# One decoder kernel: memory rows first in the DMA queues, the first projection's features turned between weight splits, and four stages without unused products

## The chip, the core and the metric

The kernel runs on one core of a Trainium2 chip. The metric is the device time of one execution, in microseconds (us). The engines are TensorE (PE in the profile; PEld is its weight load), VectorE (DVE), ScalarE (ACT), GpSimd (POOL) and SyncE (SP). SP does nothing here but issue the large transfers; ACT and POOL issue a few at the start. The kernel before takes 1924.37 us, the median of three runs (1923.10 to 1926.65).

## The reference

One sequence of 256 tokens of 1024 features, in float32, goes through four layers. What the change touches is the first of them, and the memory keys and values that two later layers read:

```
mod = silu(c) @ ada_w[layer] + ada_b[layer]          # (1024) x (1024 x 6144), two layers
sh1, sc1, g1, sh2, sc2, g2 = split(mod, 6)
h = rms_norm(x, norm1_g) * (1 + sc1) + sh1
proj = h @ even_w_in                                 # (256 x 1024) x (1024 x 3584)
rq, rk, rv, rg, aq, ak, av = split(proj)             # retention and attention inputs
rq, rk = rotary(rq), rotary(rk)
x = x + g1 * (concat(retention, attention) @ even_w_out)
...
mem_n = rms_norm(mem, mem_norm_g[l])                 # 256 memory rows, two later layers
k, v = mem_n @ ca_wk[l], mem_n @ ca_wv[l]            # (256 x 1024) x (1024 x 256) each
```

After it come a mixture of 16 experts in 4 groups, a stick-breaking attention layer with its experts, a layer with forget-gated and compressed sparse attention ("b0" in the code), a differential attention layer ("b1"), and in the last two a memory cross attention and a SwiGLU feed-forward.

## The kernel before

**Split products.** The large products are done in three passes. Each weight tile of 128 x 2048 is copied by ACT to a rounded high part (`weights_high`, line 1520), DVE subtracts that from the tile to give the low part (`weights_low`, line 2071), both in two halves of 1024 columns, and TensorE multiplies high by high, high by low and low by high (lines 722 to 724). The features are split the same way. A group of 512 output columns takes two weight tiles and 48 products of 512 columns: 24 for the features 0 to 511 (first tile, both token blocks), then 24 for the rest (second tile).

**The ring.** Weight tiles come through a ring of three slots, in two halves of 512 KB. SP asks for a half once the tile three places earlier in the plan has been split by DVE (or summed, see below), half by half; its instructions run in order, so a half that has to wait holds all later ones. The high and low parts have three slots of their own, freed when TensorE has used them.

**The modulation.** Twenty-four blocks of 512 columns of `ada_w` pass through the same ring, two tiles each. DVE sums them over the features with eight instructions per block (`ada_steps`, lines 2335 and 2342) and TensorE finishes the sum over partitions with products against ones (lines 855 and 858). Three blocks are done on TensorE (line 875). In `project`, DVE's code for the first projection puts the eight steps of a block ahead of the splits of groups 0, 1, 4, 5 and twice 6 (`ADA_EVEN`).

**The start.** ACT asks for c, the memory rows, three small constant tensors and x; POOL asks for eight small tensors, the first two gate bias rows (128 x 2048) among them. SP alternates one block of `ada_w` with one of the four memory weights. DVE sums block 0 (eight steps), then scales the memory rows by their root; TensorE transposes them for layer 0, computes its keys, transposes them for layer 1, and computes the other three products, each with one block's modulation behind it. Then ACT and DVE split both tiles of the first group, and x is transposed, scaled and shifted into features (`take_turned("a0h1", ...)`), two feature blocks at a time in turns between PE, ACT and DVE. POOL asks for the attention bias (128 x 3072), the rotary table (128 x 256) and the retention decay (128 x 1536) when the last memory values have been copied. DVE needs the rotary table at line 2231, after group 2 of the projection and the modulation behind it.

**Unused products.** `stay_busy` (line 739) multiplies a constant tile by itself into a bank that nobody reads, where TensorE would wait. It is called in many stages; each product is 128 x 512.

Of the kernel before, what the change touches and what calls it, by code (L numbers as in the profile page):

```python
# [15 lines left out]
KD = D // 128  # L16
# [164 lines left out]
def build(nc, a, out):  # L181
# [3 lines left out]
    with ctx:  # L185
# [247 lines left out]
        class Pairs:  # L433


            def __init__(self, name, P=None):

                self.name, self.wide = name, name[:2] == "ca"
                self.keys = [256, 256] if self.wide else [128, 256]
                self.width = sum(self.keys)  # L440
                self.first, self.first_out, count, self.out_banks = {
                    "a0": (0, 0, 4, [2, 3]), "b0": (4, 4, 12, [6, 7]), "ca0": (16, 12, 2, [6, 7]),
                    "ca1": (18, 14, 2, [6, 7])}[name]
                self.score_sets = 1 if name == "a0" else 2
                self.scale = 1.0 if name == "a0" else HD ** -0.5
                self.idle = {"a0": (8, 0, 0, 0), "b0": (5, 0, 0, 0)}.get(name, (4, 11, 0, 0))
                self.items = [self.item(i, P) for i in range(count)]
# [92 lines left out]
        CONSTS, MORE, LATE = 16 * 3, 16 * 8, 16 * 3  # L540
# [5 lines left out]
        def _(eng):  # L546
# [104 lines left out]
            for l in range(2):  # L651
                for i, w in enumerate(("ca_wk_2", "ca_wv_2")):
                    ada()
                    eng.dma_start(MEM_WEIGHTS[2 * l + i], cols(a[w][l], 0, 256)).then_inc(kv_loaded[2 * l + i], 16)
# [45 lines left out]
        def _(eng):  # L700
# [444 lines left out]
            turns_taken("mem0")  # L1145
            mem_keys(0)
            turn("mem1", lambda i, tb: NB[:, tb, i * 128:(i + 1) * 128])
            turns_taken("mem1")
            modulation((2, 3))
            mem_values(0)  # L1150
            modulation((2, 3))
            mem_keys(1)
            modulation((2, 3))
            mem_values(1)
            modulation((2, 3))
# [3 lines left out]
            turn_normed("a0h1", busy=(9, 3, 3, 3))  # L1159
# [30 lines left out]
            def in_even(j):  # L1190

                if j in (1, 2, 5):
                    modulation((2, 3))
                if j == 3:
                    eng.wait_ge(mod_taken, 6)
                    stay_busy(2, 4)
                    eng.wait_ge(a0_rotated, 1)
                    for x in range(4):
                        turn_a0(x, 256 * x)
                if j == 5:  # L1200
                    eng.wait_ge(a0_normed, 1)
# [120 lines left out]
            def in_ev(j):  # L1322
# [4 lines left out]
                if j == 4:  # L1327
                    eng.wait_ge(gates_copied, 1)
                    eng.wait_ge(cmp_dve, 1)
                    for i, t in enumerate(st["cmp"]):  # L1330
                        stay_busy(0, 4)
                        loaded(t)
                        w1 = slot(t).rearrange("p (k n) -> p k n", k=16)
                        for k in range(16):
                            mm = eng.matmul(B[2 + i][:, 0:31], w1[:, k, :], XS[i][:, k, :], start=(k == 0), stop=(k == 15))
                        mm.then_inc(*used.up())
# [160 lines left out]
        def _(eng):  # L1497
# [9 lines left out]
            eng.dma_start(X[:, :, :], a["x"].rearrange("b (t p) d -> p (b t) d", p=128)).then_inc(x_loaded, 16)  # L1507
# [22 lines left out]
            def take_turned(name, dst, affine=None, split=False):  # L1530

                first, items = turns[name]
                for i in range(items):
# [12 lines left out]
                    if split and i % 2 == 1:  # L1546
                        high_features(i - 1, 2, (x + 1) // 2)

# [275 lines left out]
            take_chunks(st["kv0"][0], lambda c: MK[:, 0, c, :])  # L1824
# [6 lines left out]
            take_chunks(st["kv0"][1], lambda c: MV[:, 0, c, :])  # L1831
            take_chunks(st["kv1"][0], lambda c: MK[:, 1, c, :])
            take_chunks(st["kv1"][1], lambda c: MV[:, 1, c, :])
            splits(tiles[st["even_in"][0][0][0]]["split"] + 2)
            eng.wait_ge(scales_ready, 1)
            take_turned("a0h1", feature, lambda i: (SCL[:, 0, i:i + 1], MOD[:, 0, i:i + 1]), True)
# [215 lines left out]
        def _(eng):  # L2052
# [36 lines left out]
            def take_turned(name, dst, affine=None, split=False):  # L2089
# [258 lines left out]
            def ada_take(j, banks, room=None):  # L2348

                l, i = j // 12, j % 12  # L2350
                if j == 16:
                    eng.wait_ge(gates_loaded, 16)
# [230 lines left out]
            ada_steps(KD)  # L2583
# [4 lines left out]
            ada_steps(KD)  # L2588
            take_turned("mem1", lambda i: MEM_HT[1][:, i, :], lambda i: (GM[:, 11, i:i + 1], None))
            ada_steps(KD)  # L2590
            ada_take(0, (2, 3))
# [8 lines left out]
            take_turned("a0h1", feature, lambda i: (SCL[:, 0, i:i + 1], MOD[:, 0, i:i + 1]), True)  # L2600
# [379 lines left out]
        def _(eng):  # L2980

            for dst, src in ((AG[:, :], a["qk_gains"]), (GB[:, 0:2, :], a["gate_bias"][0:2].partition_broadcast(128)),
                             (RW[:, :, :], cols(a["router_w"], 0, 16)), (RB[:, :], a["router_b"].partition_broadcast(128)),
# [3 lines left out]
            eng.wait_ge(copied["act"], chunks[st["kv1"][1][-1]]["done"])  # L2987
# [116 lines left out]
```

## Times and profile before

| what | us |
|---|---|
| median of three runs | 1924.37 |
| profiled execution, own time | 1924.36 |
| its span | 1922.6 |
| TensorE busy | 1788.5 (93%) |
| VectorE busy | 1264.9 (66%) |
| ScalarE busy | 1073.1 (56%) |
| unused products (line 739), 350 of them | 97.9 |

The profiled execution's own time is the median's. An instruction's start is counted from the start of the span. A busy TensorE is not one at its peak: matmuls overlap, so a product's cost in a row of products is the distance of two starts. TensorE's granted clock has two levels, 1.00 (2.4 GHz) and 0.50 (1.2 GHz).

### The profile page before, as it was taken

What the parts mean: (1) busy time and instruction counts of PE and PEld (TensorE: products, weight loads), DVE (VectorE), ACT (ScalarE), POOL (GpSimd) and SP (SyncE); (2) the same over time, 40 slices, a digit from 0 to 9 for tenths busy, and PEclk for the clock granted to TensorE, in tenths of its full rate; (3) what the DMA queues carried; (4) which work ended last, traced back from release to release, by engine and by line L of the source; (5) the groups of instructions that cost most, each with busy time, mean ns of one, the idle gap of its engine ahead of it and who ended that gap; (6) DMA issues with size and microseconds to landing.
All of it is one profiled execution on the core that took longest, in us unless ns stands there. A gap on an engine that the chain in (4) does not pass through costs nothing.

```text
span 1922.6 us, 27078 instructions
## 1 busy us (share of the span) xinstructions
PE 1788.5 (93%) x9548; PEld 1479.4 (77%) x9548; DVE 1264.9 (66%) x2000; ACT 1073.1 (56%) x1649; POOL 13.8 (1%) x29
## 2 busy tenths in 40 slices
PE   5997799999999999999999999888999998879998
PEld 4785478888886866888888688566999876669997
DVE  5686658889885756689888652755545555655454
ACT  2343247878873354578878552555444454564443
POOL 1000000000000000000000000000000000000000
PEclk9998799999999999999999998798999998999999
DMA  9876638999894935399999643122566552215652
GB/s 350 289 240 223 217 133 310 325 353 356 320 360 142 325 121 186 131 352 358 318 360 344 237 149 130 45 88 66 177 196 189 175 197 66 88 44 181 191 179 83
DMA packets 217285, 413.09 MB, mean 215 GB/s; under 512 B 13120, under 2 KB 69488, under 8 KB 216800
## 3 DMA queue, kind: packets, MB, share of 16 engines
q1 hardware_dynamic: 214176, 400.74, 60.7%
q0 software_dynamic: 1904, 8.26, 1.3%
q10 hardware_dynamic: 1120, 2.97, 0.4%
q8 instruction: 52, 0.85, 0.2%
q14 instruction: 33, 0.27, 0.0%
HBM read 410.87 MB, written 1.05 MB: 214 GB/s over the span
## 4 chain that ended last, share of the span: by engine, by line
PE 79%; DVE 11%; ACT 5%; issue 3%; DMA 2%; DVEq 0%; ACTq 0%; SPq 0%
PE banks L722 21%; PE banks L724 20%; PE banks L723 20%; DVE weights_low L2071 3%; PE banks L984 2%; PE banks L1126 2%; DVE row_gains L2342 2%; DMA weight_ring<-in_ada_w 1%; PE banks L1069 1%; PE banks L739 1%; PE banks L779 1%; PE banks L752 1%; ACT scratch L1671 1%; PE banks L875 1%; DVE x_state L2197 1%
## 5 line engine op out<-in xcount | busy, mean ns | idle before, releaser
L2071 DVE TENSOR_TENSOR weights_low<-weight_ring,weights_high 128x1024 fp32r<-128x1024 f32 (+1 forms) x656 | 772.5, 1218 | 185.9 <-ACT weights_high L1520 105.6
L722 PE MATMUL banks<-weights_high,features_parts 128*128 128x512 f32 (+1 forms) x1488 | 590.7, 397 | 19.3 <-DVE features_parts L2504 8.2
L723 PE MATMUL banks<-weights_low,features_parts 128*128 128x512 f32 (+1 forms) x1488 | 580.2, 390 | 0.0
L724 PE MATMUL banks<-weights_high,features_parts 128*128 128x512 f32 (+1 forms) x1488 | 580.1, 390 | 0.0
L1800 ACT ACTIVATE weights_high<-weight_ring 128x1024 fp32r<-128x1024 f32 x384 | 393.3, 1056 | 103.4 <-PE banks L724 65.5
L722 PEld LDWEIGHTS banks<-weights_high,features_parts 128*128 128x128 f32 x1488 | 280.9, 189 | 84.9 <-DVE weights_low L2071 16.1
L724 PEld LDWEIGHTS banks<-weights_high,features_parts 128*128 128x128 f32 x1488 | 280.4, 188 | 59.3
L723 PEld LDWEIGHTS banks<-weights_low,features_parts 128*128 128x128 f32 x1488 | 281.0, 189 | 55.2 <-issue 1.0
L1520 ACT ACTIVATE weights_high<-weight_ring 128x1024 fp32r<-128x1024 f32 (+1 forms) x176 | 176.0, 1043 | 137.9 <-PE banks L724 84.4
L722 PE MATMUL banks<-features_parts,weights_high 128*128 128x256 f32 x736 | 210.2, 286 | 1.6 <-DVE features_parts L2166 1.5
L724 PE MATMUL banks<-features_parts,weights_low 128*128 128x256 f32 x736 | 208.2, 283 | 0.0
L723 PE MATMUL banks<-features_parts,weights_high 128*128 128x256 f32 x736 | 208.2, 283 | 0.0
L722 PEld LDWEIGHTS banks<-features_parts,weights_high 128*128 128x128 f32 x736 | 141.2, 192 | 3.7 <-issue 2.2
L723 PEld LDWEIGHTS banks<-features_parts,weights_high 128*128 128x128 f32 x736 | 141.2, 192 | 0.7
L724 PEld LDWEIGHTS banks<-features_parts,weights_low 128*128 128x128 f32 x736 | 141.1, 192 | 0.0
L2016 ACT ACTIVATE weights_high<-weight_ring 128x1024 fp32r<-128x1024 f32 x96 | 96.0, 1048 | 55.8 <-PE banks L724 55.8
L2342 DVE SCALAR_TENSOR_TENSOR row_gains<-weight_ring,c_features,row_gains 128x512 f32<-128x512 f32 x133 | 99.9, 751 | 30.3 <-DMA weight_ring<-in_ada_w 22.3
L739 PE MATMUL banks<-fill 128*128 128x512 f32 x350 | 97.9, 427 | 0.3 <-DVE modulation L2371 0.3
L2903 DVE TENSOR_TENSOR projected<-projected,banks 128x256 f32<-128x256 f32 x44 | 18.5, 421 | 104.6 <-PE banks L724 104.6
L739 PEld LDWEIGHTS banks<-fill 128*128 128x128 f32 x350 | 68.9, 204 | 18.1 <-issue 4.2
L1671 ACT ACTIVATE scratch<-scratch,row_shifts 128x128 f32<-128x128 f32 (+1 forms) x80 | 36.2, 454 | 73.6 <-DVE row_shifts L2263 73.6
L1993 ACT ACTIVATE features_parts<-projected 128x512 fp32r<-128x512 f32 x22 | 13.9, 630 | 74.7 <-PE banks L724 74.7
(371 smaller groups left out, 1625.2 us busy)
## 6 DMA issues: line engine op xcount, KB each, us to landing
weight_ring<-in_exp_w_gate SPq DMA_DIRECT2D x128, 512.0 KB, 5.2
weight_ring<-in_exp_w_up SPq DMA_DIRECT2D x128, 512.0 KB, 5.1
weight_ring<-in_exp_w_down SPq DMA_DIRECT2D x128, 512.0 KB, 5.3
weight_ring<-in_ada_w SPq DMA_DIRECT2D x96, 512.0 KB, 5.4
weight_ring<-in_ffn_wg SPq DMA_DIRECT2D x44, 512.0 KB, 4.2
weight_ring<-in_ffn_wu SPq DMA_DIRECT2D x44, 512.0 KB, 4.7
weight_ring<-in_ffn_wd SPq DMA_DIRECT2D x44, 512.0 KB, 4.2
weight_ring<-in_even_w_in SPq DMA_DIRECT2D x28, 512.0 KB, 6.0
```

The lines of the kernel that those rows point to most:

```text
L722: eng.matmul(dst, lh, rh, start=first, stop=False, **kw)
L723: eng.matmul(dst, lh, rl, start=False, stop=False, **kw)
L724: mm = eng.matmul(dst, ll, rh, start=False, stop=last, **kw)
L739: eng.matmul(B[bank][:, :], FILL[:, :], FILL[:, :].unsqueeze(1).to_broadcast([128, 4, 128]), start=True, stop=True, skip_group_check=True)
L984: mm = eng.matmul(B[4 + b][:, k * 128:(k + 1) * 128], NB[:, tb, (4 * b + k) * 128:(4 * b + k + 1) * 128], SEL[:, tb, :], start=(tb == 0), ...
L1126: mm = eng.matmul(B[4 + q % 4][:, 0:256], left, right, start=i == 0, stop=i == len(steps) - 1)
L1520: eng.activation(half_of(high(s), i, t["size"]), half_of(slot(t["n"]), i, t["size"]), ACT.Copy)\
L1671: eng.activation(p, p, ACT.Exp, scale=-1.0, bias=small(SHIFT, t)[:, i:i + 1], accum_out=small(SUMS, t)[:, i:i + 1]).then_inc(probs_ready, 1)
L1800: eng.activation(half_of(high(t["split"]), x), half_of(slot(t["n"]), x), ACT.Copy)\
L2016: eng.activation(half_of(high(t["split"]), x), half_of(slot(t["n"]), x), ACT.Copy)\
L2071: V(half_of(low(s), i, size), half_of(slot(n), i, size), half_of(high(s), i, size).bitcast(F32), ALU.subtract)\
L2342: ins = eng.scalar_tensor_tensor(out=acc, in0=w, scalar=CF[:, k:k + 1], in1=acc, op0=ALU.mult, op1=ALU.add)
```

## The change

It has four parts.

1. SP's and ACT's requests at the start are in another order. x is asked for by SP and no longer by ACT. SP asks for the first tile of block 0, waits until the memory rows have landed, and goes on with the first memory weights, the second tile, the next memory weights and x; the other two memory weights follow blocks 1 and 2. POOL waits for the memory rows before its small tensors; the gate bias rows are no longer among them and are asked for just ahead of the attention bias, and all four now wait for the last copy of group 0 of the first projection.
2. At the start TensorE transposes the memory rows for both layers before any keys; DVE sums four steps of block 0 before it scales the memory rows, four after, and scales x before it sums block 1.
3. ACT splits the first tile of the first group ahead of the features of x and the second after the first four features. DVE splits the first tile ahead of them; its own `take_turned` takes the new argument and has no call of it in its body, so the second tile's low parts come with the splits of `project`.
4. The unused products go from four stages: 18 among the transposes of x, 4 ahead of the rotated heads' transposes (with a wait for a modulation that stood before them), 8 behind the first attention ("a0"), 5 behind the attention "b0", and 8 beside the compression products of "b0" (line 1335).

```diff
@@ class Pairs
-                self.idle = {"a0": (8, 0, 0, 0), "b0": (5, 0, 0, 0)}.get(name, (4, 11, 0, 0))
+                self.idle = {"a0": (0, 0, 0, 0), "b0": (0, 0, 0, 0)}.get(name, (4, 11, 0, 0))
@@ SP
-            for l in range(2):
-                for i, w in enumerate(("ca_wk_2", "ca_wv_2")):
-                    ada()
-                    eng.dma_start(MEM_WEIGHTS[2 * l + i], cols(a[w][l], 0, 256)).then_inc(kv_loaded[2 * l + i], 16)
+            def mem_weights(l, i):
+
+                w = ("ca_wk_2", "ca_wv_2")[i]
+                eng.dma_start(MEM_WEIGHTS[2 * l + i], cols(a[w][l], 0, 256)).then_inc(kv_loaded[2 * l + i], 16)
+
+            first = st["ada"][0]
+            load(first[0], cols(a["ada_w"][0], 0, 512, 0, 4), 4)
+            eng.wait_ge(mem_loaded, 16)
+            mem_weights(0, 0)
+            load(first[1], cols(a["ada_w"][0], 0, 512, 4, 4), 4)
+            loaded_chunks[0] += 1
+            mem_weights(0, 1)
+            eng.dma_start(X[:, :, :], a["x"].rearrange("b (t p) d -> p (b t) d", p=128)).then_inc(x_loaded, 16)
+            ada()
+            mem_weights(1, 0)
+            ada()
+            mem_weights(1, 1)
+            ada()
@@ TensorE
             turn_normed("mem0")
-            turns_taken("mem0")
-            mem_keys(0)
             turn("mem1", lambda i, tb: NB[:, tb, i * 128:(i + 1) * 128])
             turns_taken("mem1")
-            modulation((2, 3))
-            mem_values(0)
-            modulation((2, 3))
-            mem_keys(1)
-            modulation((2, 3))
-            mem_values(1)
-            modulation((2, 3))
+            for l in range(2):
+                mem_keys(l)
+                modulation((2, 3))
+                mem_values(l)
+                modulation((2, 3))
...
-            turn_normed("a0h1", busy=(9, 3, 3, 3))
+            turn_normed("a0h1")
...
                 if j == 3:
-                    eng.wait_ge(mod_taken, 6)
-                    stay_busy(2, 4)
                     eng.wait_ge(a0_rotated, 1)
...
                     for i, t in enumerate(st["cmp"]):
-                        stay_busy(0, 4)
                         loaded(t)
@@ ScalarE
-            eng.dma_start(X[:, :, :], a["x"].rearrange("b (t p) d -> p (b t) d", p=128)).then_inc(x_loaded, 16)
...
-            def take_turned(name, dst, affine=None, split=False):
+            def take_turned(name, dst, affine=None, split=False, midway=None):
...
                     if split and i % 2 == 1:
                         high_features(i - 1, 2, (x + 1) // 2)
+                    if midway is not None and i == 3:
+                        midway()
...
-            splits(tiles[st["even_in"][0][0][0]]["split"] + 2)
+            s0 = tiles[st["even_in"][0][0][0]]["split"]
+            splits(s0 + 1)
             eng.wait_ge(scales_ready, 1)
-            take_turned("a0h1", feature, lambda i: (SCL[:, 0, i:i + 1], MOD[:, 0, i:i + 1]), True)
+            take_turned("a0h1", feature, lambda i: (SCL[:, 0, i:i + 1], MOD[:, 0, i:i + 1]), True, lambda: splits(s0 + 2))
@@ VectorE
-            def take_turned(name, dst, affine=None, split=False):
+            def take_turned(name, dst, affine=None, split=False, midway=None):
...
-                if j == 16:
-                    eng.wait_ge(gates_loaded, 16)
+                if j in (4, 16):
+                    eng.wait_ge(gates_loaded, 16 * (1 + j // 12))
...
-            ada_steps(KD)
+            ada_steps(4)
             normalise(lambda tb: PR[:, tb * D:(tb + 1) * D])
             eng.wait_ge(consts_loaded, CONSTS)
             eng.tensor_copy(FILL[:, :], ones).then_inc(fill_ready, 1)
             take_turned("mem0", feature, lambda i: (GM[:, 10, i:i + 1], None))
-            ada_steps(KD)
             take_turned("mem1", lambda i: MEM_HT[1][:, i, :], lambda i: (GM[:, 11, i:i + 1], None))
-            ada_steps(KD)
-            ada_take(0, (2, 3))
+            ada_steps(4)
             eng.wait_ge(turned, turns["mem1"][0] + KD)
             eng.wait_ge(x_loaded, 16)
             norm_x()
             ada_steps(KD)
-            for j in (1, 2, 3):
+            for j in range(4):
                 ada_take(j, (2, 3))
-            splits(tiles[st["even_in"][0][0][0]]["split"] + 2)
+                if j < 2:
+                    ada_steps(KD)
+            s0 = tiles[st["even_in"][0][0][0]]["split"]
+            splits(s0 + 1)
@@ GpSimd
+            eng.wait_ge(mem_loaded, 16)
...
-            eng.wait_ge(copied["act"], chunks[st["kv1"][1][-1]]["done"])
+            eng.wait_ge(copied["act"], chunks[st["even_in"][0][1][1]]["done"])
+            eng.dma_start(GB[:, 0:2, :], a["gate_bias"][0:2].partition_broadcast(128)).then_inc(gates_loaded, 16)
             for dst, src in ((bias, a["rel_bias"]), (EARLY, a["early"]), (SCR[:, 0:RET_HEADS, :], a["decay"])):
```

**VectorE, from the last modulation of the start to the first features of x.** `weights_low` are the low halves of weight tiles, `features_parts` the low parts of the features. Before:

```order
L2371 TENSOR_TENSOR modulation<-banks,ada_bias_features 128x4 x3
L2376 SCALAR_TENSOR_TENSOR gain_times_scale<-modulation,feature_gains 128x8
L2071 TENSOR_TENSOR weights_low<-weight_ring,weights_high 128x1024 x4
L2105 TENSOR_SCALAR qk_features<-banks,gain_times_scale,modulation 128x256
L2087 TENSOR_TENSOR features_parts<-qk_features,features_parts 128x512
```

After:

```order
L2379 TENSOR_TENSOR modulation<-banks,ada_bias_features 128x4 x2
L2384 SCALAR_TENSOR_TENSOR gain_times_scale<-modulation,feature_gains 128x8
L2079 TENSOR_TENSOR weights_low<-weight_ring,weights_high 128x1024 x2
L2113 TENSOR_SCALAR qk_features<-banks,gain_times_scale,modulation 128x256
L2095 TENSOR_TENSOR features_parts<-qk_features,features_parts 128x512
```

Two of the four low halves, those of the first group's second tile, have left this place.

**VectorE, from the last features of x on.** The rows at `row_gains<-weight_ring` are the eight sums of modulation block 4. Before:

```order
L2087 TENSOR_TENSOR features_parts<-qk_features,features_parts 128x512
L2602 TENSOR_SCALAR qk_norm_gains<-qk_norm_gains 128x1
L2335 TENSOR_SCALAR row_gains<-weight_ring,c_features 128x512
L2342 SCALAR_TENSOR_TENSOR row_gains<-weight_ring,c_features,row_gains 128x512 x7
L2071 TENSOR_TENSOR weights_low<-weight_ring,weights_high 128x1024 x4
```

After:

```order
L2095 TENSOR_TENSOR features_parts<-qk_features,features_parts 128x512
L2611 TENSOR_SCALAR qk_norm_gains<-qk_norm_gains 128x1
L2343 TENSOR_SCALAR row_gains<-weight_ring,c_features 128x512
L2350 SCALAR_TENSOR_TENSOR row_gains<-weight_ring,c_features,row_gains 128x512 x7
L2079 TENSOR_TENSOR weights_low<-weight_ring,weights_high 128x1024 x6
```

The two low halves now stand behind the eight sums, at the head of a row of six; the other four are those of group 1, as before.

**SP, the requests of the start.** `weight_ring<-in_ada_w` are halves of modulation tiles, four to a block. Before:

```order
L563 DMA weight_ring<-in_ada_w 128x2x512 x4
L654 DMA aux<-in_ca_wk 128x8x256
L563 DMA weight_ring<-in_ada_w 128x2x512 x4
L654 DMA scratch<-in_ca_wv 128x8x256
L563 DMA weight_ring<-in_ada_w 128x2x512 x4
L654 DMA qk_features<-in_ca_wk 128x8x256
L563 DMA weight_ring<-in_ada_w 128x2x512 x4
L654 DMA projected<-in_ca_wv 128x8x256
L563 DMA weight_ring<-in_even_w_in 128x2x512 x4
```

After:

```order
L563 DMA weight_ring<-in_ada_w 128x2x512 x2
L654 DMA aux<-in_ca_wk 128x8x256
L563 DMA weight_ring<-in_ada_w 128x2x512 x2
L654 DMA scratch<-in_ca_wv 128x8x256
L663 DMA x_state<-in_x 128x2x1024
L563 DMA weight_ring<-in_ada_w 128x2x512 x4
L654 DMA qk_features<-in_ca_wk 128x8x256
L563 DMA weight_ring<-in_ada_w 128x2x512 x4
L654 DMA projected<-in_ca_wv 128x8x256
L563 DMA weight_ring<-in_ada_w 128x2x512 x4
L563 DMA weight_ring<-in_even_w_in 128x2x512 x4
```

The first memory weights stand between the two tiles of block 0, and x (from ACT's queue) and the second memory weights stand ahead of block 1.

## Rows read from the trace of the kernel before

**Rows 1.** Timeline of the start: start us, us, engine line, op [idle before].

```profile
12.48 1.06 ACT L1584 ACTIVATE normed<-projected 128x1024 f32<-128x1024 f32 x1 [5.08 <-DMA projected<-in_mem]
...
14.70 0.29 ACT L1588 ACTIVATE root<-square_sums,epsilon 128x2 f32<-128x2 f32 x1
...
20.28 1.42 DVE L2123 TENSOR_SCALAR normed<-projected,reciprocal_root 128x1024 f32<-128x1024 f32 x2
...
21.85 3.65 PE L752 MATMUL banks<-constants,normed 128*128 128x128 f32 x16 [21.85 <-DVE normed L2123]
```

**Rows 2.** DMA queues, 8 to 9 us: packets, MB, share of 16 engines.

```profile
q0 software_dynamic: 31, 0.25, 60.5%
q10 hardware_dynamic: 30, 0.12, 29.9%
q1 hardware_dynamic: 30, 0.05, 12.1%
```

**Rows 3.** Timeline of DVE, 54 to 102 us.

```profile
63.19 4.63 DVE L2071 TENSOR_TENSOR weights_low<-weight_ring,weights_high 128x1024 fp32r<-128x1024 f32 x4 [0.21 <-ACT weights_high L1520]
...
75.94 5.68 DVE L2342 SCALAR_TENSOR_TENSOR row_gains<-weight_ring,c_features,row_gains 128x512 f32<-128x512 f32 x7
...
81.54 4.63 DVE L2071 TENSOR_TENSOR weights_low<-weight_ring,weights_high 128x1024 fp32r<-128x1024 f32 x4
```

**Rows 4.** Chain of waits, 0 to 220 us: start us, us, what.

```profile
83.95 0.50 PE banks L722
...
96.75 0.86 PE banks L855 x2
108.53 0.87 PE banks L855 x2
...
110.03 2.50 DVE normed L2231 x4
```

**Rows 5.** The weight ring's transfers, 78 to 108 us.

```profile
DMA to landing us min/median/max: 3.7/5.7/6.5
```

**Rows 6.** DMA queues, 66 to 67 us.

```profile
q0 software_dynamic: 35, 0.43, 101.5%
```

**Rows 7.** DMA queues, 68 to 69 us.

```profile
q0 software_dynamic: 77, 0.30, 73.9%
q1 hardware_dynamic: 30, 0.06, 15.8%
```

**Rows 8.** Stretches: us; PE, PEld, DVE, ACT, POOL busy; PEclk, DMA share, GB/s.

```profile
86.00:88.00 2.00, 2.00 (x7) 1.52 (x6) 1.86 (x4) 0.00 (x0) 0.00 (x0) 0.50 1.01 303
88.00:90.00 2.00, 2.00 (x8) 1.61 (x7) 1.82 (x4) 0.00 (x0) 0.00 (x0) 0.78 1.00 350
...
188.00:190.00 2.00, 0.56 (x3) 0.56 (x4) 1.97 (x9) 0.00 (x0) 0.00 (x0) 0.50 1.04 400
...
194.00:196.00 2.00, 2.00 (x6) 1.10 (x5) 1.50 (x3) 0.84 (x2) 0.00 (x0) 0.83 0.49 170
```

**Rows 9.** Timeline of PE behind the first attention and behind the attention b0.

```profile
232.54 3.53 PE L739 MATMUL banks<-fill 128*128 128x512 f32 x8
236.63 0.47 PE L722 MATMUL banks<-weights_high,features_parts 128*128 128x512 f32 x1 [0.55 <-DVE weights_low L2071]
...
1261.04 1.43 PE L739 MATMUL banks<-fill 128*128 128x512 f32 x5
...
1290.12 3.69 PE L779 MATMUL banks<-projected,x_state 128*128 128x128 f32 x16 [1.92 <-DVE projected L2204]
```

**Rows 10.** PEclk behind that last gap, columns as in rows 8.

```profile
1291.00:1292.00 1.00, 1.00 (x6) 0.97 (x6) 0.45 (x2) 0.16 (x1) 0.00 (x0) 0.50 0.00 0
```

**Rows 11.** Chain of waits, 1140 to 1300 us.

```profile
1169.44 0.91 PE banks L739 x4
1170.34 3.49 PE banks L1335 x32
1173.83 1.36 PE banks L739 x4
1175.19 6.67 PE banks L1335 x32
1181.86 0.59 PE banks L722
...
1263.42 0.50 PE banks L722
```

More of the change, by code:

```diff
@@ L537, in diff_turned_at @@
             return SCRF[:, 1536 + 384 * (t % 2):1920 + 384 * (t % 2)]
-        CONSTS, MORE, LATE = 16 * 3, 16 * 8, 16 * 3
+        CONSTS, MORE, LATE = 16 * 3, 16 * 7, 16 * 3
         block = ctx.enter_context(nc.Block())
@@ L1823, in _ @@
             take_turned("mem0", feature, lambda i: (GM[:, 10, i:i + 1], None))
-            take_chunks(st["kv0"][0], lambda c: MK[:, 0, c, :])
             take_turned("mem1", lambda i: MEM_HT[1][:, i, :], lambda i: (GM[:, 11, i:i + 1], None))
@@ L1830, in _ @@
             take_root(SS, TB, D)
-            take_chunks(st["kv0"][1], lambda c: MV[:, 0, c, :])
-            take_chunks(st["kv1"][0], lambda c: MK[:, 1, c, :])
-            take_chunks(st["kv1"][1], lambda c: MV[:, 1, c, :])
-            splits(tiles[st["even_in"][0][0][0]]["split"] + 2)
+            for l in range(2):
+                take_chunks(st[f"kv{l}"][0], lambda c: MK[:, l, c, :])
+                take_chunks(st[f"kv{l}"][1], lambda c: MV[:, l, c, :])
+            s0 = tiles[st["even_in"][0][0][0]]["split"]
+            splits(s0 + 1)
             eng.wait_ge(scales_ready, 1)
-            take_turned("a0h1", feature, lambda i: (SCL[:, 0, i:i + 1], MOD[:, 0, i:i + 1]), True)
+            take_turned("a0h1", feature, lambda i: (SCL[:, 0, i:i + 1], MOD[:, 0, i:i + 1]), True, lambda: splits(s0 + 2))
             P0 = pview(EVEN_IN)
@@ L2595, in _ @@
             ada_steps(KD)
-            for j in (1, 2, 3):
+            for j in range(4):
                 ada_take(j, (2, 3))
-            splits(tiles[st["even_in"][0][0][0]]["split"] + 2)
+                if j < 2:
+                    ada_steps(KD)
+            s0 = tiles[st["even_in"][0][0][0]]["split"]
+            splits(s0 + 1)
             eng.wait_ge(scales_ready, 1)
-            take_turned("a0h1", feature, lambda i: (SCL[:, 0, i:i + 1], MOD[:, 0, i:i + 1]), True)
+            take_turned("a0h1", feature, lambda i: (SCL[:, 0, i:i + 1], MOD[:, 0, i:i + 1]), True, lambda: splits(s0 + 2))
             eng.wait_ge(more_loaded, MORE)
@@ L2980, in _ @@
         def _(eng):
-            for dst, src in ((AG[:, :], a["qk_gains"]), (GB[:, 0:2, :], a["gate_bias"][0:2].partition_broadcast(128)),
-                             (RW[:, :, :], cols(a["router_w"], 0, 16)), (RB[:, :], a["router_b"].partition_broadcast(128)),
+            eng.wait_ge(mem_loaded, 16)
+            for dst, src in ((AG[:, :], a["qk_gains"]), (RW[:, :, :], cols(a["router_w"], 0, 16)), (RB[:, :], a["router_b"].partition_broadcast(128)),
                              (POS[:, :, :], a["cmp_pos"]), (W2[:, :], a["cmp_w2"]), (PI[:, :], a["positions_fm"]),
```

## The prediction

> **What bounds the kernel now.** I read three views: the timeline of the start, then the chain of waits over the places that the change touches, then the DMA queues and the granted clock microsecond by microsecond. TensorE is busy for 93% of the span, and the chain runs through it nearly everywhere, so a microsecond counts where TensorE's work moves. The reader is to see four things. TensorE starts at 21.85 us; the memory rows are there at 12.5, their root at 15.0, but VectorE scales them only at 20.3, behind the eight sums of block 0 [rows 1]. Between 63.2 and 86 VectorE splits, turns features, sums block 4 for 6.2 us and splits again without rest [rows 3], and TensorE waits for it at 83.95, the start of group 1 [rows 4]. TensorE then sets the end of group 1 (96.75), of group 2 (108.5) and the start of VectorE's rotation at 110.03 [rows 4]; I take that moment as the end of the start's account, since what follows hangs on it alike in both kernels. And the clock falls to 0.50 after short gaps [rows 8 to 10], which is what unused products may prevent.
>
> **A, the earlier start.** At 8 to 9 us three queues moved 0.42 MB: POOL's 0.25, ACT's 0.12, SP's 0.05 [rows 2]. The gate bias rows (128 x 2048 floats, 1.05 MB) leave POOL's queue: 1.05/0.42 = 2.5 us less ahead of the memory rows. SP's wait takes some more out of their way, I say 0.5: they land at 9.5 instead of 12.5. Squares and root take 2.5 [rows 1], VectorE has only four sums ahead and is done: scaling starts at 12.1, and TensorE 1.6 later, as now: 13.7 instead of 21.85, 8.2 gained. TensorE then works 40.8 us to the last modulation before group 0. The work stays; one wait for copies goes, about 1.0. VectorE's first low half moves from T = 63.2 [rows 3] to T = 54.0. The data keep up: 15.6 MB lie ahead of group 0's first tile, at 0.38 to 0.42 MB/us from 3 us on there by 40 to 44, some 6 us later with the pause for the memory rows, a slower spell of small tensors and the small rows of the memory weights. A is -9.2, between -7 (late constants or a late block 3) and -10.5.
>
> **B, the second tile behind the sums.** From T to the sums of block 4 VectorE now takes 12.2 us, four low halves of 1.16 in it [rows 3]. Two leave (-2.3), and ScalarE's two high halves in the middle of the features hold it up for about 1.4: T+11.3. The eight sums take 6.2 and stand ahead of the second tile's low halves, 2.4: TensorE may begin that tile at T+20.0. It finished the first near T+12 and stood. After such a stand it restarts at half clock: at 189.44 it restarts (0.56 us of work in 188 to 190) and the clock is back near 194.7 [rows 8], 5.2 us at half speed, 2.6 lost. The tile's 24 products take 5.5 (group 2, 48 products, 97.6 to 108.5 [rows 4], 0.227 each), so group 1 begins at T+28.0 where it now begins at T+20.8. Today's group 1 holds 1.8 of low clock (86 to 90, [rows 8]); the new one has 10.9. It ends at T+38.9, its modulation at T+39.8 = 93.8; now at 97.6 = T+34.4. B is +5.4, between +4 and +7. What hides nothing here: the ring. Group 1's first tile takes the second tile's place, so it can be asked for only at T+18.8 to 20.0; with 3.7 to 5.7 to land [rows 5], a high and a low half (2.3), it is ready at T+26.4, 1.6 under TensorE. If that cover goes, each microsecond counts.
>
> **C, POOL's transfers in a new place.** They now go with the last memory copy, at 62.5, and run while VectorE is the bound. In the changed kernel they go with the last copy of group 0, about 82.9, and are 128 x (2048 + 3072 + 256 + 1536) floats, 3.54 MB. At 66 to 67 POOL's queue moved 0.43 MB and the ring's nothing [rows 6]; at 68 to 69 it was 0.30 against 0.06 [rows 7]. So 3.54/0.42 = 8.4 us go before the ring's. Behind POOL's waiting instruction stand only these. In the ring lie then the rest of block 5 and group 2's first tile, whose place comes free at 81.6 and 83.0: undisturbed it would be there at 88.5, now at 97; with high and low 99.3. TensorE wants it at 93.8. C is +5.5, between 0 (the ring gets its share) and +9 (late parts of block 5 hold VectorE's in-order splits too). **D**, the restart at half clock behind that stand, as above: +2.6, between 0 and 2.6. Group 2 then ends at 99.3 + 10.9 + 2.6 = 112.8, and the rotation starts at 114.3: A + B + C + D = +4.3.
>
> The Trainium skill, "DMA: Bandwidth & Descriptors", section on queues, rings and completion order, says that an engine takes turns between its queues packet by packet. The counts at 8 to 9 us agree (31, 30 and 30 packets for very unequal bytes, [rows 2]); 66 to 67 does not (35 and none). By the rule with packets of 12 KB against 2 KB the ring would get a seventh all the time, the tile would come about half a microsecond sooner, and the sum would be 0.5 less.
>
> **E, the unused products.** The 18 among x's transposes only filled waits: 0, their clock effect is in B. The four ahead of the rotated heads cost 0.9 on TensorE, but VectorE's sums and splits end later there: 0, at best -0.9. Behind the first attention eight products run from 232.54 to 236.1 at half clock (3.53 us for eight, 0.43 each), and the first real product, held by a low half until 236.63, runs at full clock at once [rows 9]. Without them it restarts cold: 1.6 (the spell of 86 to 90) to 2.6 lost, I take +2.1; 0 if the clock holds. Behind b0 five products cover 1.4 of a stand of 2.4 up to 1263.42 [rows 9, 11]. A gap of 1.92 ahead of 1290.12 was followed by 0.50 [rows 9, 10], so I take a spell there: +1.6, between 0 and 1.7. Beside the compression the eight stand on the chain: 0.91 + 1.36 go, but the clock fell under this row of narrow products (32 in 3.49, then 32 in 6.67 [rows 11]) and would fall somewhat nearer its start in work: -2.3, between -3.0 and -1.0. Together +1.4.
>
> **The sum.** +4.3 + 1.4 = +5.7 on the profiled execution's own 1924.36 (span 1922.6, 1.8 around it), which is the median of the runs: 1930.1 us.
>
> **The rivals.** *The ring keeps its share.* C and D vanish: -9.2 + 5.4 = -3.8, with +1.4 it is -2.4: 1922.0, not slower. It decides from the point where group 2's first tile lands before 91.5. For it: the request is made about when POOL's is, and POOL's queue took two microseconds to come to full rate; against it: rows 6 and 7. *The clock holds over the new gaps.* Then B is +2.8, D 0, TensorE waits the 2.6 in C instead (8.1), E is -3.0: -9.2 + 2.8 + 8.1 - 3.0 = -1.3: 1923.1. Against it: rows 8 and 10. *Both:* -9.2 + 2.8 - 3.0 = -9.4: 1915. *The stall deepens.* Late halves of block 5 hold VectorE, which stands in order ahead of group 2's splits, and the second tile of group 2 stands too: 4 to 6 more, 1935. *The start does not move,* because the constants, now behind nothing but slow small tensors, land as late as before: with A at -4, 1935 too; the rows speak against it, and it is counted with the one before.
>
> **How the numbers follow.** Forecast 0.43, ring keeps its share 0.27, clock holds 0.12, both 0.06, deeper stall or late start 0.12. The range of 8 in 10 is 1918 to 1935; the forecast's own is 1926 to 1934. A measurement here can tell about 0.2% (3.9 us) from no change. Slower by more: four fifths of the forecast and all of the deeper stall, 0.46. Faster by more: "both", a third of the second case and a third of the third, 0.19. The rest, 0.35, is within it.
>
> **What would show it.** TensorE's first transposes near 13.7 and VectorE's first low half near 54 (A). A stand of 7 us or more in TensorE between two tiles of group 0, ended by a low half that has eight sums ahead of it (B). A second stand near 94 to 99 ended by the high half of group 2's first tile, which waits for its DMA, with POOL's queue near 0.4 MB/us and the ring's near nothing (C), and half clock behind both (B, D). The rotation near 114. Half clock in the first products behind the first attention and behind b0, and a compression stage about 2.3 us shorter. I am wrong if the rotation starts before 110, if the tile of group 2 lands by 91, or if the clock stays at 1.00 in both places of E.

## The result, and the profile after

The changed kernel takes 1933.66 us, the median of six runs (1928.12 to 1941.00), against 1925.22 for six of the kernel before. The ratio is 1.0042 [1.0023, 1.0060]: slower by 8.1 us of 1925, between 4.4 and 11.6. Put on the chip a second time beside other kernels it was 1.0055 [1.0041, 1.0068]. The forecast, 1930.1 or a ratio of 1.0030, lies in the first interval and 2.1 us under the lower end of the second. The profiled execution of it is the quickest of its six runs, 1928.12 (span 1926.3), 3.8 above the one of before; its stages are compared with that in mind.

Below, "us by the ratio" is a kernel's ratio less one, times 1925. It compares a kernel with the runs of before that share its chip, which medians taken on different days do not.

The timeline of the start (start us, us, engine line, op, idle before):

```profile
8.69 1.06 ACT L1592 ACTIVATE normed<-projected 128x1024 f32<-128x1024 f32 x1 [1.98 <-DMA projected<-in_mem]
...
11.44 1.42 DVE L2131 TENSOR_SCALAR normed<-projected,reciprocal_root 128x1024 f32<-128x1024 f32 x2
...
13.01 5.68 PE L766 MATMUL banks<-constants,normed 128*128 128x128 f32 x32 [13.01 <-DVE normed L2131]
```

TensorE starts 8.8 us sooner [rows 1]. The chain of waits says what limits the start now: x, asked for at 10.95, took 13.95 us to land, and behind it stand its scaling and the eight sums of block 1, for which TensorE waits at 35.36.

```profile
10.95 13.95 DMA x_state<-in_x
24.93 2.20 ACT projected L1592 x4
27.77 1.42 DVE normed L2131 x2
...
35.36 1.05 PE banks L872 x8
```

VectorE from there to group 2 (this answers to [rows 3]):

```profile
54.31 2.36 DVE L2079 TENSOR_TENSOR weights_low<-weight_ring,weights_high 128x1024 fp32r<-128x1024 f32 x2 [0.21 <-ACT weights_high L1526]
...
65.89 5.68 DVE L2350 SCALAR_TENSOR_TENSOR row_gains<-weight_ring,c_features,row_gains 128x512 f32<-128x512 f32 x7
...
71.49 2.35 DVE L2079 TENSOR_TENSOR weights_low<-weight_ring,weights_high 128x1024 fp32r<-128x1024 f32 x2
...
97.83 1.22 DVE L2079 TENSOR_TENSOR weights_low<-weight_ring,weights_high 128x1024 fp32r<-128x1024 f32 x1 [5.45 <-ACT weights_high L1526]
```

The first low half has come from 63.19 to 54.31. The second tile's two stand behind the sums, at 71.49. TensorE waits for both places. The third row is another stand, behind the first attention, where eight unused products used to be:

```profile
73.89 0.80 PE L736 MATMUL banks<-weights_high,features_parts 128*128 128x512 f32 x1 [6.43 <-DVE weights_low L2079]
...
99.11 0.80 PE L736 MATMUL banks<-weights_high,features_parts 128*128 128x512 f32 x1 [5.65 <-DVE weights_low L2079]
...
239.39 0.76 PE L736 MATMUL banks<-weights_high,features_parts 128*128 128x512 f32 x1 [4.01 <-DVE weights_low L2079]
```

The first product after each stand takes 0.76 to 0.80 us, where the one at 236.63 behind the eight unused products took 0.47 [rows 9]. Which transfer is behind the stand at 99.11, the chain tells: the tile of group 2 was asked for at 85.16 and needed 11.56 us, where it used to take 3.7 to 6.5 [rows 5].

```profile
85.16 11.56 DMA weight_ring<-in_even_w_in
96.74 1.06 ACT weights_high L1526
97.83 1.24 DVE weights_low L2079
99.11 0.80 PE banks L736
111.61 0.87 PE banks L869 x2
113.12 2.50 DVE normed L2239 x4
```

And the DMA queues show who had the engines, here in the microsecond from 94 (packets, MB, share of 16 engines; q0 is POOL's queue):

```profile
q0 software_dynamic: 29, 0.36, 85.6%
q1 hardware_dynamic: 28, 0.06, 15.5%
```

The two queues got nearly the same number of packets, and POOL's moved six times the bytes. The Trainium skill, "DMA: Bandwidth & Descriptors", section "Queues, rings and completion order", says that an engine takes turns between queues packet by packet; the counts here agree (29 and 28; 43 and 39 in the microsecond from 91). The prediction had this as its second reading, at half a microsecond less.

The rotation starts at 113.12, before at 110.03 [rows 4]: +3.1, forecast +4.3.

Stretches behind the first attention (columns as in [rows 8]):

```profile
236.00:238.00 2.00, 0.00 (x0) 0.00 (x0) 1.48 (x3) 2.00 (x3) 0.00 (x0) 0.50 0.02 4
238.00:240.00 2.00, 0.61 (x2) 0.55 (x3) 2.00 (x3) 2.00 (x3) 0.00 (x0) 0.50 0.33 90
240.00:242.00 2.00, 2.00 (x6) 1.60 (x5) 2.00 (x3) 1.47 (x2) 0.00 (x0) 0.50 0.78 268
242.00:244.00 2.00, 2.00 (x6) 1.53 (x5) 1.68 (x2) 0.00 (x0) 0.00 (x0) 0.50 0.90 280
244.00:246.00 2.00, 2.00 (x7) 1.58 (x7) 0.00 (x0) 0.00 (x0) 0.00 (x0) 0.67 0.95 320
```

TensorE is idle until 239.39, and full work from 240 goes on at 0.50 for some 5 us more. The clock had fallen before this gap, in both kernels (near 225 before, near 228 now), among the attention's own short products; what differs is its return, near 235.7 with the eight products and 245.3 without. The compression, at last, is one row now, 8.68 where [rows 11] had 12.4 with its eight unused products. The clock fell about 5.5 us after the stage's start, 4.9 before:

```profile
1175.06 8.68 PE L1342 MATMUL banks<-normed,weight_ring 128*128 128x31 f32 x64
```

### The profile page after: what moved, and what is told of

The parts are those of the page before. It is cut to its first block, busy times and chain, and to the rows that moved or that the text cites. A ratio compares the mean times of both kernels' runs of the same rounds, so it can differ in the third digit from the quotient of the medians.

```text
span 1926.3 us, 26992 instructions
## 1 busy us (share of the span) xinstructions
PE 1783.0 (93%) x9505; PEld 1473.6 (76%) x9505; DVE 1265.5 (66%) x2000; ACT 1073.5 (56%) x1649; POOL 14.1 (1%) x29
## 4 chain that ended last, share of the span: by engine, by line
PE 77%; DVE 11%; ACT 6%; DMA 3%; issue 3%; SPq 0%; DVEq 0%; ACTq 0%
PE banks L736 21%; PE banks L738 20%; PE banks L737 20%; DVE weights_low L2079 3%; PE banks L998 2%; DVE row_gains L2350 2%; PE banks L1083 1%; DMA weight_ring<-in_even_w_in 1%; PE banks L753 1%; ACT weights_high L1526 1%; ACT scratch L1679 1%; PE banks L889 1%; PE banks L793 1%; DVE x_state L2205 1%; PE banks L1140 1%
## 5 line engine op out<-in xcount | busy, mean ns | idle before, releaser
L753 PE MATMUL banks<-fill 128*128 128x512 f32 x307 | 84.2, 423 | 0.3 <-DVE modulation L2379 0.3
L753 PEld LDWEIGHTS banks<-fill 128*128 128x128 f32 x307 | 60.4, 203 | 16.1 <-issue 3.7
```

Source lines behind the costliest of these rows:

```text
L753: eng.matmul(B[bank][:, :], FILL[:, :], FILL[:, :].unsqueeze(1).to_broadcast([128, 4, 128]), start=True, stop=True, skip_group_check=True)
```

## The experiments

Two readings of the loss stand against each other. The prediction's: two late placements (the second tile's low halves, POOL's four transfers) turn a gain of 9 us into a loss of 4, and the unused products add little. The rival: the unused products are the cause, and the start is nearly even. Each kernel below ran beside the kernel before on the same chip, five to twelve runs each. Behind each expectation stand the median and range of its runs in us, the ratio with its 95% interval, and where it bears on the start the start of the rotation in its profile.

**e1: POOL's four transfers back behind the last memory copy.** The changed kernel with

```diff
-            eng.wait_ge(copied["act"], chunks[st["even_in"][0][1][1]]["done"])
+            eng.wait_ge(copied["act"], chunks[st["kv1"][1][-1]]["done"])
```

> The changed kernel with one edit: POOL's four transfers (3.54 MB) are asked for when the last memory values are copied, as before the change. My theory (they starve the ring and delay group 2's first tile): TensorE's stand near 94 to 99 us and the half clock behind it go, the rotation starts near 105 instead of 113, and the kernel is 8 us shorter (5.5 for the stand, 2.6 for the restart). Rival (the tile is late because its place in the ring is free late, at 85): the stand stays, the time is within 2 us of the changed kernel's.

1927.75 (1919.59 to 1931.05), 1.0013 [0.9999, 1.0027], rotation 105.76. In the trace the transfers go at 51.6, TensorE still stands before the second tile, and the stand before group 2 is gone:

```profile
51.63 0.54 POOL L2997 DMA_DIRECT2D row_gains<-in_gate_bias  x1 [38.25 <-ACT mem_values L1572]
...
73.14 0.79 PE L736 MATMUL banks<-weights_high,features_parts 128*128 128x512 f32 x1 [8.14 <-DVE weights_low L2079]
```

By the ratios it is 5.6 us under the changed kernel's first measurement and 8.1 under its second: C and D (8.1 in the forecast) are there.

**e2: the low halves of the second tile between the features.** VectorE's `take_turned` calls the argument that ScalarE's calls:

```diff
                         low_features(i - 3, 2)
+                    if midway is not None and i == 5:
+                        midway()
```

> The changed kernel with one edit: DVE splits the second tile of group 0 between the features, behind the low parts of features 2 and 3, as ACT does with the high parts. My theory (the eight sums stand in its way): TensorE's stand between the two tiles of group 0 (66 to 74) goes, group 1 starts near 75 to 76 instead of 80; POOL's transfers then start near 73 and hit the tiles of block 5 instead of group 2's; the rotation starts near 105 to 107, 6 to 8 us earlier. Rival (VectorE's total work sets group 1 and not its order): group 1 starts at 79 to 80 as in the changed kernel and the gain is under 2 us.

1931.83 (1928.06 to 1934.65), 1.0044 [1.0027, 1.0060], rotation 109.60. Nothing that a measurement can tell from the changed kernel: the same ratio as its first measurement, 2.1 us under its second. The expectation, 6 to 8 us sooner at the rotation, was missed; it is 3.5 sooner in the trace. The trace shows why:

```profile
75.83 0.50 PE L736 MATMUL banks<-weights_high,features_parts 128*128 128x512 f32 x1 [2.42 <-DVE weights_low L2079]
...
94.95 0.79 PE L736 MATMUL banks<-weights_high,features_parts 128*128 128x512 f32 x1 [7.08 <-DVE weights_low L2079]
```

The first stand shrinks from 6.43 to 2.42 and the second grows from 5.65 to 7.08: group 0 ends sooner, but POOL's transfers wait for its last copy and delay group 2's tile all the same (asked for at 78.08, it took 14.48 us). The wait behind the one removed took part of the gain over; where the 3.5 us left at the rotation went is not shown.

**e3: both.**

> Both edits, POOL's transfers early and VectorE's second tile between the features. My theory: the parts add, since nothing else holds the start up: group 1 near 76, group 2 near 87 to 88, the rotation near 100, 12 to 13 us less than the changed kernel (about 1921). Rival (block 4's second tile, asked for at 55.5, now comes behind POOL's transfers and holds VectorE's sums until 66 or later): less than 9 us gained.

1922.72 (1912.60 to 1925.83), 0.9982 [0.9966, 0.9999], rotation 98.65. One stand of 2.44 is left and no second. The edit gives 11.6 us by the ratio against the changed kernel's first measurement, 14.1 against its second; its two halves alone gave 5.6 and nothing, or 8.1 and 2.1. That the whole is more than its halves is no more than likely by the times: with intervals of some 3 us either way on each ratio the difference, 4 to 6 us, is at the edge of the noise. At the rotation the halves gave 7.4 and 3.5, the whole 14.5. The rotation is 14.5 sooner than in the changed kernel's trace:

```profile
74.15 0.50 PE L736 MATMUL banks<-weights_high,features_parts 128*128 128x512 f32 x1 [2.44 <-DVE weights_low L2079]
...
224.91 0.76 PE L736 MATMUL banks<-weights_high,features_parts 128*128 128x512 f32 x1 [4.01 <-DVE weights_low L2079]
```

But against the kernel before it gains only 3.5 us, though its rotation starts 11.4 sooner. By the medians something behind the start takes 8 us back, in spite of a cheaper compression. The profile shows half of that: its span is 7.6 under the one of before. It is of one of five runs from 1912.60 to 1918.27 with a mean clock of 0.959 to 0.963; the other seven, 1922.30 to 1925.83, had 0.955 or 0.956, and no profile shows where those lost it. The second row shows the stand behind the first attention, followed by half clock.

**e8: e3 with the unused products of the two attentions back,** eight and five:

```diff
-                self.idle = {"a0": (0, 0, 0, 0), "b0": (0, 0, 0, 0)}.get(name, (4, 11, 0, 0))
+                self.idle = {"a0": (8, 0, 0, 0), "b0": (5, 0, 0, 0)}.get(name, (4, 11, 0, 0))
```

> The two edits, and the eight unused products behind the first attention and the five behind b0 put back; the other 30 stay away. My theory: 3.7 us less than the kernel with both edits (2.1 behind the first attention, 1.6 behind b0), near 1917 to 1918, and runs closer together than the changed kernel's. Rival (these products were without effect, and the spread of the changed kernel's runs has another cause): the same as with both edits within 1 us.

1912.52 (1910.07 to 1914.47), 0.9944 [0.9928, 0.9959]. It beats both kernels: 10.8 us under the kernel before. The thirteen products are worth 7.3 us here, with an interval apart from e3's; the forecast's terms for them sum to 3.7. Behind the first attention TensorE waits 0.60 us and goes on at full clock:

```profile
221.73 3.48 PE L753 MATMUL banks<-fill 128*128 128x512 f32 x8
225.81 0.47 PE L736 MATMUL banks<-weights_high,features_parts 128*128 128x512 f32 x1 [0.60 <-DVE weights_low L2079]
```

**e9 and e10: e3 with the eight alone, and with the five alone** (the same line with `(8, 0, 0, 0)` and zeros, or zeros and `(5, 0, 0, 0)`).

> The changed kernel with both of its late placements mended (as e3: POOL's four transfers behind the last memory copy, VectorE's low half of the second tile between the features) and, of the unused products, the eight behind the first attention back. Without any the ratio to the kernel before was 0.9982, with these eight and the five behind b0 it was 0.9944. If each of the two stages gives what the prediction took for it (2.1 and 1.6), this one lies 2 us below the first, 0.997. If the eight give most of the 7 us, because the first products behind the attention run at full clock from their start instead of at half clock for 5 to 6 us, it is 0.9955 or lower. If neither gives much alone and the 7 us are how half-clock stretches fall elsewhere, it stays at 0.998 and e10 too.

> The same with the five products behind b0 back and not the eight behind the first attention. By the prediction's sizes 1.6 us below the kernel without either, 0.9974; if the eight carry nearly all, 0.998; if the five carry it (the trace without them has half clock for 3 to 4 us before 1269), 0.9955.

The eight: 1915.11 (1910.36 to 1923.93), 0.9950 [0.9931, 0.9968]. The five: 1918.48 (1913.31 to 1923.73), 0.9976 [0.9965, 0.9988]. So the eight give 6.2 us and the five 1.2, which sum to e8's 7.3. The interval of the eight just touches e3's (0.9968 and 0.9966), so their size is uncertain by some 5 us; the five's overlaps e3's, and their effect alone isn't shown. Term E had 2.1 for the eight and 1.6 for the five.

Only 2.7 us of the eight's 6.2 lie where they stand: in e3 the products from 224.91 to 230.3 run at half clock, which loses half of 5.4. Some of the rest may lie hundreds of microseconds later. This table counts the microseconds at half clock, from windows of one microsecond, in the profiled executions of the two kernels and the ten experiments. It holds the three stretches ahead of b0 in which the two groups differ:

| stretch | with the eight: before, e4, e5, e8, e9 | without: after, e7, e1, e2, e3, e6, e10 |
|---|---|---|
| at the first attention's end | 10.2 in all five | 17.1 in all seven |
| beginning between 593 and 609 | 0 in all five | 0 in after, 3.4 in six |
| from 762 to 780 on | 6.8, 6.8, 13.7, 6.8, 10.2 | 10.2, 10.2, 17.1, 10.2, 13.7, 13.7, 10.2 |

e9 and e10 in the same stretch of their 1913.3 us show the second line (columns as in [rows 8]; the stage comes 1.6 us later in e10); first e9, with the eight:

```profile
592.00:596.00 4.00, 3.70 (x25) 3.15 (x26) 1.94 (x4) 2.11 (x4) 0.00 (x0) 1.00 0.11 47
```

and e10, without:

```profile
592.00:596.00 4.00, 2.14 (x9) 2.10 (x10) 2.12 (x4) 1.07 (x3) 0.00 (x0) 0.73 0.53 223
```

The stand ahead of these products is the same in both, 2.18 us; the first eight take 1.09 in e9 (first row) and 1.97 in e10:

```profile
592.30 1.09 PE L766 MATMUL banks<-constants,normed 128*128 128x128 f32 x8 [2.18 <-DVE normed L2133]
593.86 1.97 PE L766 MATMUL banks<-constants,normed 128*128 128x128 f32 x8 [2.18 <-DVE normed L2133]
```

The means of the last two lines of the table differ by 2.9 and 3.3 us of half clock, up to 3.1 lost; with the 2.7 that is 5.8, near the measured 6.2. This is no account of it, though. From 1000 us on e9's profile has 91.6 us of half clock and e3's 78.9, more in e9 above all near b0, and the spans of the two differ by only 1.7. That the eight shorten the kernel is what e9 against e3 says by the runs; that they do it by the stretches near 600 and 770 is argued from twelve single profiles, and by what path a gap at 221 to 225 would bring a fall near 600 stays open.

**e4: the kernel before without the eight compression products.**

```diff
                     for i, t in enumerate(st["cmp"]):
-                        stay_busy(0, 4)
                         loaded(t)
```

> The kernel before with one edit: the eight unused products beside the compression products of b0 are gone. My theory: they stand on the chain with 2.27 us and the clock falls a little sooner in work, so 2.3 us less (1 to 3). Rival (the clock falls as much earlier as the products took, and the narrow products run at half clock for longer): no gain, within 0.5 us.

1921.42 (1917.15 to 1922.74), 0.9981 [0.9972, 0.9990]: 3.7 us gained, forecast 2.3. The stage goes from 12.4 us to 9.09:

```profile
1168.83 9.09 PE L1334 MATMUL banks<-normed,weight_ring 128*128 128x31 f32 x64
1177.73 0.77 PE L722 MATMUL banks<-weights_high,features_parts 128*128 128x512 f32 x1
```

**e6: the kernel before without the eight and the five.**

```diff
-                self.idle = {"a0": (8, 0, 0, 0), "b0": (5, 0, 0, 0)}.get(name, (4, 11, 0, 0))
+                self.idle = {"a0": (0, 0, 0, 0), "b0": (0, 0, 0, 0)}.get(name, (4, 11, 0, 0))
```

> The kernel before with one edit: the eight unused products behind the first attention and the five behind b0 are gone. My theory: TensorE restarts at half clock in both places, 2.1 and 1.6 us, so 3.7 more. Rival (the clock in these places falls or holds by chance, whatever fills them): within 1 us of before, and half clock in neither place or in only one of them.

1928.14 (1923.21 to 1935.62), 1.0026 [1.0012, 1.0040]: 5.0 us lost, between 2.3 and 7.7; forecast 3.7. With e4 the three stages would give +1.3 in the kernel before, which is what the prediction had for E (1.4). The two terms in it are each larger than forecast, by amounts inside their intervals.

**e5: the changed kernel with all its unused products back** (18 among x's transposes, four with their wait ahead of the rotated heads, the eight, the five, the eight at the compression), so the new order of the start alone:

```diff
-            turn_normed("a0h1")
+            turn_normed("a0h1", busy=(9, 3, 3, 3))
...
                 if j == 3:
+                    eng.wait_ge(mod_taken, 6)
+                    stay_busy(2, 4)
                     eng.wait_ge(a0_rotated, 1)
...
                     for i, t in enumerate(st["cmp"]):
+                        stay_busy(0, 4)
                         loaded(t)
...
-                self.idle = {"a0": (0, 0, 0, 0), "b0": (0, 0, 0, 0)}.get(name, (4, 11, 0, 0))
+                self.idle = {"a0": (8, 0, 0, 0), "b0": (5, 0, 0, 0)}.get(name, (4, 11, 0, 0))
```

> The changed kernel with all 43 unused products back, so that only the start's order differs from the kernel before. My theory: the start alone costs what the rotation's start shows, 3 to 4 us more than before, and the runs lie as close together as the kernel before's (5 us apart and not 13), 1.4 us or more under the changed kernel. Rival (the start's order spreads the runs): the same median and spread as the changed kernel.

1927.64 (1924.50 to 1932.60), 1.0022 [1.0012, 1.0032], rotation 110.42. The new order costs 4.2 us by the ratio, between 2.3 and 6.2 (A to D: 4.3), so the rival's nearly even start is refuted, and the start is about half of the whole loss. The runs lie 8.1 us apart, where 5 was expected. Both stands are there:

```profile
72.56 0.79 PE L736 MATMUL banks<-weights_high,features_parts 128*128 128x512 f32 x1 [8.32 <-DVE weights_low L2082]
96.14 0.50 PE L736 MATMUL banks<-weights_high,features_parts 128*128 128x512 f32 x1 [4.39 <-DVE weights_low L2082]
```

Its own rotation is only 0.4 later than before's, and the changed kernel's 3.1 (e7's 5.0). So one profile of the start is uncertain by some 2 us, and the closeness of 4.2 to 4.3 is in part luck: this profile doesn't show the 4.2 at the rotation. What the 18 products do shows in the first tile of group 0; first the changed kernel, then e5:

```profile
57.00:65.00 8.00, 7.04 (x20) 5.25 (x21) 3.87 (x8) 5.77 (x9) 0.00 (x0) 0.57 0.35 127
57.00:65.00 8.00, 7.23 (x34) 5.59 (x32) 4.58 (x10) 4.70 (x7) 0.00 (x0) 1.00 0.22 80
```

They keep the clock at 1.00 there, and TensorE only stands longer for it (8.32 for 6.43): the second tile starts 19.6 us behind the first low half in both.

**e7: the changed kernel once more, beside e4 to e6.**

> The changed kernel once more, for a second profile of it. The first profile is of its fastest run of six (1928.1, median 1933.7). My theory: the start is the same within 1 us (rotation near 113), and the runs above 1930 hold more stretches at half clock behind the places where the unused products are gone. Rival: the longer runs have a longer start, with group 2's tile landing later.

1935.22 (1931.79 to 1936.36), 1.0055 [1.0041, 1.0068], rotation 115.02, 1.9 later than in the first profile, where within 1 was expected; the spans differ by 5.2. So both the expectation and its rival hold in part: there is more half clock behind b0 (10.3 us near 1261 to 1276, 3.4 in the first profile), and the start is longer too. Against e5 on the same chip the 43 unused products are worth 6.4 us by the ratio (3.9 by the first measurement): E as a whole, forecast 1.4.

## Why the prediction was right, and where its terms were not

The sign, the size and the mechanism of the start came out as forecast. Taking the unused products away cost more than it gave them: 3.9 to 6.4 us of the loss against 1.4.

**A** (TensorE at 13.7, first low half at 54.0): 13.01 and 54.31. What the working took for granted, that the data keep up, didn't quite hold: x's landing is on the chain. The first low half comes at 52.3 (e1), 53.0 (e5) and 53.1 us (e3), where no half clock falls between 36 and 44; at 54.3 (the changed kernel) and 54.7 (e2) with 3.4 us of it there, and at 56.3 (e7) with 6.8. A was -8.9 in the first profile, forecast -9.2.

**B** (second tile at T + 20.0): it started at 73.89, T + 19.6, behind a stand of 6.43 that the low halves behind eight sums end. Group 1 and its modulation end at 93.5, forecast 93.8. TensorE's last product ahead of the stand ended at T + 13.2 and not T + 12, since the clock was at half already from 57 to 65, which the working didn't have; the stand hid it. e2 and e3 show that the place of the two low halves is the cause of the stand.

**C** (tile of group 2 at 97, TensorE at 99.3): 96.7 and 99.11. Two errors cancel in this: its place came free, and POOL's transfers went, 2.2 us later than worked out (85.2 for 83.0 and 85.14 for 82.9), and it landed in 11.6 us and not in 14. e1, which moves POOL's transfers alone, takes the stand away. The rival in which the ring keeps its share fell: it kept its share of packets and not of bytes.

**D** (2.6 for the restart): the modulation behind group 2 starts 12.5 us after the group, and 10.9 in [rows 4]: 1.6. It was mis-sized by one, and this is nearly all of the difference between +4.3 and +3.1 at the rotation.

**E** (+1.4): the step that was off. Compression -2.3, measured -3.7 (e4, between -1.9 and -5.4, so the forecast is inside). The eight behind the first attention +2.1: the profile shows 2.5 of it up to the router (271.9 against 266.3, less the 3.1 of the start), e9 against e3 6.2 in all. I had priced a gap by the cold spell right behind it, and taken for granted that what follows hangs on it alike; most of the traces without the eight show more half clock also near 600 and 770. The five behind b0 +1.6: 1.2 (e10), not told from none. At b0 the spell came (1266 to 1269), but the one of 1291 in [rows 10] is gone in exchange, and both profiles hold about 13.6 us of half clock from 1240 to 1330. The 18 and the four, at zero, weren't measured alone; e7 less e5 (+6.4) leaves 6.4 - 6.2 - 1.2 + 3.7 = 2.7 for them, and by the first measurement 0.2, so whether they are free is open.

The sum of E's parts as measured, 6.2 + 1.2 - 3.7 = 3.7, with 4.2 for the order, is 7.9 against the 8.1 measured. With each part uncertain by 2 to 5 us, and 10.6 in the second measurement, so close a sum is luck. Of the rivals, "the clock holds" fell at both places, and "the stall deepens" by 4 to 6 didn't come: one stand before group 2, of 5.65.

## What to carry to other kernels

An earlier start is worth what the next engine in line makes of it: 8.8 us gained at the first transposes were gone at the start of group 2, because two low halves were put behind eight sums and bulky transfers ahead of a tile that is needed at once. Two delays in series can hide each other: in e2 the second stand grew when the first shrank, and the edit that seemed to do nothing there stood in the one that gave 11.6. So such an edit is tried again with its neighbour mended. Unused products that fill a wait which is there anyway can be worth more than the cold spell that they avoid (thirteen of them 7.3 us here, 5.0 in the kernel before), while the eight beside the compression, where work was ready, cost at least about their length (2.3 us of products, 3.7 gained without them). Look at what ends the wait before adding or taking one.

## What the runs showed of the hardware

The same stand can be followed by full clock in one profile and by half clock in another, as the one of 2.18 near 600 in e9 and e10. Without the eight products the stretch at the first attention's end is 6.9 us longer in seven executions of seven, and six of them have a further 3.4 us at half clock near 600, which none of the five with them has. Over the rest of the kernel no such order is seen: from 1000 us on the sum is 81.3 to 91.6 with the eight and 78.9 to 96.2 without. Behind b0 the stretch from 1240 to 1330 holds 13.6 to 13.7 us of half clock in all five executions with the five products (before, e4, e5, e8, e10), and between 10.3 and 23.9 in the seven without: 10.3 twice, 13.7 twice, 23.9 three times. One of those is e9, where a stand of 2.20 ahead of 1251.05 is followed by products at 0.63 us until 1256.8:

```profile
1251.05 0.79 PE L736 MATMUL banks<-weights_high,features_parts 128*128 128x512 f32 x1 [2.20 <-DVE features_parts L2285]
1251.64 0.63 PE L737 MATMUL banks<-weights_low,features_parts 128*128 128x512 f32 x1
...
1256.76 0.57 PE L737 MATMUL banks<-weights_low,features_parts 128*128 128x512 f32 x1
1257.17 0.40 PE L738 MATMUL banks<-weights_high,features_parts 128*128 128x512 f32 x1
```

In the changed kernel a stand of 2.31 ahead of 1265.32 cost less: its first product took 0.50 and half clock held from 1266 to 1269. So one profile prices a clock effect badly. The runs scatter too: over 12.9 us in the changed kernel, 11.5 in e1, 13.2 in e3 and 12.4 in e6, without the eight and the five, against 4.4 in e8, 5.6 in e4 and 8.1 in e5, with both; e9 with the eight alone has 13.6 and e10 with the five alone 10.4. e2 and e7 (6.6 and 4.6, of six and five runs) do not fit, so that this is no more than a tendency.
